# Expert rows turned by VectorE in 32x32 squares, gate and up products on column quarters, and a slot map made by products

## The reference, cut to what matters

```
M, D = 2080, 1024          # tokens, features;  w_gate, w_up: 1024x512;  w_down: 512x1024
gate = g_w * softmax(top_v);  expert = grp * 8 + top_i        # two experts for each token
# rows grouped by expert, each group padded to whole blocks
hdn = silu(xb @ w_gate[e]) * (xb @ w_up[e])                   # for each block xb of rows
yr  = hdn @ w_down[e]
out[token] += gate * yr[row of that token]
```

## Time and profile before

| | us |
|---|---|
| median of 3 runs | 3718.13 |
| lowest and highest | 3712.8, 3718.2 |
| profiled execution, its own time | 3718.09 |
| its span | 3716.3 |
| PE busy in the span | 2902.1 |
| DVE busy | 1572.8 |
| ACT busy | 1129.7 |
| POOL busy | 731.6 |

### The profile page before, as it was taken

The page is one execution under the profiler, slowest core; times in us unless marked ns, Lnnn a source line. Parts: engine busy times, 40 slices in busy tenths (PEclk is TensorE's granted clock), DMA queues, the critical chain, the costliest instruction groups (busy, mean ns, idle before and its releaser), DMA issues. The chain is left out here.

```text
span 3716.3 us, 44002 instructions
## 1 busy us (share of the span) xinstructions
PE 2902.1 (78%) x14656; PEld 1423.4 (38%) x14657; DVE 1572.8 (42%) x3624; ACT 1129.7 (30%) x2012; POOL 731.6 (20%) x858
## 2 busy tenths in 40 slices
PE   7999988925864657777774669992899999999940
PEld 3545353513432234555553434551333333333310
DVE  1145677886751578887643323332000000000025
ACT  1132452643431469865551211110111111111111
POOL 1404130301203323223314200003100000000024
PEclk9999999966777868889997779995999999999975
DMA  5011010002223101100006443321787668777747
GB/s 188 31 39 59 19 36 32 33 17 70 79 57 98 54 27 36 33 21 18 12 10 221 175 147 108 113 83 19 253 281 270 231 218 282 263 273 252 243 153 261
DMA packets 235196, 447.52 MB, mean 120 GB/s; under 512 B 49516, under 2 KB 86622, under 8 KB 235054
## 3 DMA queue, kind: packets, MB, share of 16 engines
q1 hardware_dynamic: 194158, 334.49, 26.4%
q0 software_dynamic: 27616, 89.49, 7.2%
q10 hardware_dynamic: 13280, 21.77, 1.8%
HBM read 359.98 MB, written 85.69 MB: 120 GB/s over the span
## 5 line engine op out<-in xcount | busy, mean ns | idle before, releaser
L773 PE MATMUL pj_cm<-pj_xT,pj_w 128*64 128x512 f32 (+1 forms) x1216 | 395.6, 600 | 5.8 <-ACT pj_xst L670 3.2
L2818 PE MATMUL ex_pgu<-ex_wgu,ex_xT 128*64 128x512 f32 x1344 | 297.7, 595 | 0.0
L2818 PE MATMUL ex_pgu<-pre_down_wgu,ex_xT 128*64 128x512 f32 x1312 | 293.2, 600 | 0.7 <-ACT ex_xT L2738 0.7
L2783 DVE TENSOR_TENSOR ex_hid<-ex_sg,ex_pgu 128x256 f32<-128x256 f32 x83 | 35.0, 421 | 596.6 <-ACT ex_sg L2742 596.6
L773 PEld LDWEIGHTS pj_cm<-pj_xT,pj_w 128*64 128x64 f32 (+1 forms) x1216 | 153.4, 163 | 240.4 <-issue 230.3
L2002 PE MATMUL ap_SB<-keep_kT,ap_qs 64*128 64x512 f32 (+3 forms) x640 | 169.2, 621 | 93.6 <-DVE ap_m L1934 74.7
L2013 PE MATMUL ap_TB<-keep_const,ap_L 128*128 128x128 f32 x1088 | 177.1, 306 | 69.2 <-ACT ap_PT L1795 48.5
L1783 ACT ACTIVATE ap_L<-ap_L,ap_nm 128x128 f32<-128x128 f32 (+15 forms) x128 | 153.2, 1197 | 174.1 <-DVE ap_nm L1939 170.4
L696 ACT ACTIVATE pj_U<-pj_sc,pj_cand 128x512 bf16<-128x512 f32 (+4 forms) x155 | 183.3, 1184 | 66.5 <-DVEq L517 66.4
L496 DVE TENSOR_SCALAR_CACHE_REDUCE pj_U<-pj_sc,pj_cand 128x384 bf16<-128x384 f32 (+9 forms) x182 | 194.7, 1103 | 14.2 <-issue 0.5
L2013 PEld LDWEIGHTS ap_TB<-keep_const,ap_L 128*128 128x128 f32 x1088 | 130.3, 153 | 149.5 <-ACT ap_L L1783 59.3
(11 more groups left out here) (521 smaller groups left out, 4790.9 us busy)
## 6 DMA issues: line engine op xcount, KB each, us to landing
pre_down_wgu<-in_w_gate SPq DMA_DIRECT2D x16, 2048.0 KB
pre_down_wgu<-in_w_up SPq DMA_DIRECT2D x16, 2048.0 KB
pre_down_wd<-in_w_down SPq DMA_DIRECT2D x16, 2048.0 KB, 8.9
ex_wgu<-in_w_gate SPq DMA_DIRECT2D x16, 2048.0 KB
ex_wgu<-in_w_up SPq DMA_DIRECT2D x16, 2048.0 KB
ex_wd<-in_w_down SPq DMA_DIRECT2D x16, 2048.0 KB
yslot<-ex_y ACTq DMA_DIRECT2D x166, 128.0 KB, 6.0
pj_x<-in_x_prompt SPq DMA_DIRECT2D x16, 512.0 KB, 5.1
```

Of the source, the lines that this page charges most:

```text
L773: mm = pe.matmul(cm[u % 2][cols * n:cols * n + cols, 0:width_], w[:, k, c0:c0 + cols], xT[:, k, 0:width_], start=(k == 0), stop=(k == KD - 1))
L2783: v.tensor_tensor(hid[:], sg[:], pgu[:, DE // 2:DE], ALU.mult).then_inc(sm["hid_ok"], 1)
L2818: mm = pe.matmul(pgu[BR * t:BR * t + BR, :], xT[:, k % 4, k // 4, :], wgu[par][:, k, :, 256 * t:256 * t + 256], start=(k == 0), stop=(k == ...
```

## The change

- **Layout of the normed rows.** `xn` is written by four `scalar_tensor_tensor` of 256 elements instead of one of 1024, with its features in another order, so that a quarter of a stored row holds the 32-wide pieces which one group of 32 partitions needs. `wr` is loaded by 16 transfers in the matching order instead of two. `w_down` is loaded by four transfers, one for each chunk, with its rows in another order.
- **Slot map.** The 34 scatters, the table `slot_tok` and its loads go. VectorE makes, for each of 34 columns of slots, a one-hot of the row in its block and a one-hot of the block, the latter times the token number. PE multiplies and sums them in 34 products, and VectorE makes the row numbers (eight small operations) from the result. Two small constant rows are loaded by SP.
- **Blocks.** POOL gathers 128 quarter rows of 1 KB twice for a block. VectorE turns them in 32x32 squares by one `transpose`, and the gated products by another, both from SBUF to SBUF. PE's transposes and ACT's two copies go. `gate_up` works on 32 rows at a time (`hh`), for each chunk four products of 32 stationary columns by 256 moving ones, one on each quarter of the array's columns; silu and the multiply work on these halves too. `down` keeps its eight products.

```
 def load_down(sp, io, buf, e, sem):
-    sp.dma_start(buf[:], io["w_down"][0, e].rearrange("(k p) f -> p k f", p=P)).then_inc(sem, 16)
+    rows = io["w_down"][0, e].rearrange("(q k j) f -> k q j f", q=4, j=32)
+    for k in range(DE // P):
+        sp.dma_start(buf[:, k, :], rows[k]).then_inc(sem, 16)
 (mix_out, SP)
-            sp.dma_start(wr[:, :, 0:NGRP], io["w_router_group"][0].rearrange("(k p) n -> p k n", p=P)).then_inc(sm["w_in"], 16)
-            sp.dma_start(wr[:, :, 8:LG], io["w_router_expert"][0].rearrange("(k p) n -> p k n", p=P)).then_inc(sm["w_in"], 16)
+            for c0, c1, name in ((0, NGRP, "w_router_group"), (8, LG, "w_router_expert")):
+                by_part = io[name][0].rearrange("(m c q j) n -> q m c j n", m=2, c=4, q=4)
+                for k in range(KD):
+                    sp.dma_start(wr[:, k, c0:c1], by_part[k // 2, k % 2]).then_inc(sm["w_in"], 16)
 (mix_out, POOL)
-            for t in range(NT):
-                rows = P if t < TILES else DEC
-                for k in range(2):
-                    pool.indirect_dma_start(io["slot_tok"], bass.IndirectOffsetOnAxis(ap=keep["slot"][0:rows, 2 * t + k:2 * t + k + 1], axis=0),
-                                            toki[0:rows, t:t + 1], None).then_inc(sm["scat"], 16)
-            pool.wait_ge(sm["scat"], 16 * 2 * NT)
 (mix_out, VectorE: one tile's xn, and the map)
-                    v.scalar_tensor_tensor(xn[r, par, :], xr[r, par, :], rstd[r, :], n2w[r, :], ALU.mult, ALU.mult).then_inc(sm["xn_ok"], 1)
+                    for q in range(4):
+                        part = lambda a_: a_.rearrange("p (k q j) -> p k q j", q=4, j=32)[:, :, q, :]
+                        ins = v.scalar_tensor_tensor(xn[r, par, 256 * q:256 * q + 256].rearrange("p (k j) -> p k j", j=32), part(xr[r, par, :]),
+                                                     rstd[r, :], part(n2w[r, :]), ALU.mult, ALU.mult)
+                    ins.then_inc(sm["xn_ok"], 1)
...
+            for c in range(2):
+                sl = slice(q * c, q * c + q)
+                v.tensor_tensor(onerow[:, sl, :], bc(rowio[:].unsqueeze(1), [P, q, BR]), bc(lowf[:, sl].unsqueeze(2), [P, q, BR]), ALU.is_equal)
+                for i in range(q * c, q * c + q):
+                    r = slice(0, rows_of(i // 2))
+                    v.tensor_scalar(oneblk[r, i, :], blkio[r, :], blkf[r, i:i + 1], keep["tok"][r, i // 2:i // 2 + 1], ALU.is_equal, ALU.mult).then_inc(sm["oh_ok"], 1)
+            v.wait_ge(sm["map_ok"], 1)
+            for q in range(4):
+                for hh in range(2):
+                    v.tensor_scalar(keep["rows"][32 * q:32 * q + 32, hh, 0:MAXBLK], pl[32 * hh:32 * hh + 32, 0:MAXBLK], 4.0, float(q), ALU.mult, ALU.add)
 (mix_out, PE)
+            for i in range(2 * NT):
+                r = slice(0, rows_of(i // 2))
+                pe.wait_ge(sm["oh_ok"], i + 1)
+                mm = pe.matmul(pl[0:BR, 0:MAXBLK], onerow[r, i, :], oneblk[r, i, :], start=(i == 0), stop=(i == 2 * NT - 1))
 (experts, POOL)
-                pool.indirect_dma_start(xg[:], None, halves, bass.IndirectOffsetOnAxis(ap=cur[:], axis=0)).then_inc(sm["xg_in"], 16)
+                for hh in range(2):
+                    pool.indirect_dma_start(xg[:, hh, :], None, quarters, bass.IndirectOffsetOnAxis(ap=cur[:, hh:hh + 1], axis=0)).then_inc(sm["xg_in"], 16)
 (experts, VectorE; a block is hidden(b), rows_done(b - 1), drain, turn_hidden(b))
+            def turn_rows(b):
+                v.wait_ge(sm["xg_in"], 32 * b + 32)
+                v.transpose(xT[:].rearrange("p k h t -> p h k t"), xg[:].rearrange("p h (k t) -> p h k t", t=32)).then_inc(sm["xt_ok"], 1)
             def hidden(b):
+                v.drain()
+                for hh in range(2):
+                    v.wait_ge(sm["sg_ok"], 2 * b + hh + 1)
+                    ins = v.tensor_tensor(hid[:, hh, :], sg[:, hh, :], pgu[hh][:, P:2 * P], ALU.mult)
+                ins.then_inc(sm["hid_ok"], 1)
+                turn_rows(b + 1)
+            def turn_hidden(b):
+                v.transpose(hT[:].rearrange("p k h t -> p h k t"), hid[:].rearrange("p h (k t) -> p h k t", t=32)).then_inc(sm["h_ok"], 1)
 (experts, PE; a block is gate_up(b), down(b - 1))
-                for k in range(KD):
-                    for t in range(2):
-                        mm = pe.matmul(pgu[BR * t:BR * t + BR, :], xT[:, k % 4, k // 4, :],
-                                       wgu[par][:, k, :, 256 * t:256 * t + 256], start=(k == 0), stop=(k == KD - 1))
+                for hh in range(2):
+                    for k in range(KD):
+                        for q in range(4):
+                            mm = pe.matmul(pgu[hh][32 * q:32 * q + 32, 0:2 * P], xT[:, k, hh, :],
+                                           wgu[par][:, k, :, P * q:P * q + P], start=(k == 0), stop=(k == KD - 1))
+                    mm.then_inc(sm["gu_ok"], 1)
```

More of the change, by code:

```diff
@@ L43 @@
 MAXBLK = 98
+SHIFT = BR.bit_length() - 1
 GROUP = 4
@@ L146 @@
 PICK, PK = picks()
+KEYROW = np.arange(MAXBLK, dtype=np.float32)[None, :].copy()
 SHIFTS = np.arange(BITS - 1, -1, -1)
@@ L2665, in experts @@
         wd = [keep["ew_d"], a.sb("wd", [P, DE // P, D])]
[L2666 to L2673 removed]
+        rows = keep["rows"]
+        cur = a.sb("cur", [P, 2], I32)
+        xg = a.sb("xg", [P, 2, D // 4])
+        xT = a.sb("xT", [P, KD, 2, 32])
+        sg = a.sb("sg", [P, 2, P])
+        hid = a.sb("hid", [P, 2, P])
+        hT = a.sb("hT", [P, DE // P, 2, 32])
         y = a.sb("y", [P, D // 2])
         zero = a.sb("zero", [BR, D])
[L2676 to L2677 removed]
+        pgu, py = [a.ps(f"pgu{n}") for n in range(2)], a.ps("py")
+        names = ("xg_in", "xt_ok", "gu_ok", "sg_ok", "hid_ok", "h_ok", "y_ok", "y_cp", "y_st", "zero_ok", "tail_st", "go")
         sm = {n: a.sem(n) for n in names}
@@ L2680, in experts @@
         block = a.block()
-        halves = io["xn2"].rearrange("r (h c) -> (r h) c", h=2)
+        quarters = io["xn2"].rearrange("r (q c) -> (r q) c", q=4)
         def over_blocks(eng, first, rest):
@@ L2699, in _ @@
         def _(sp):
-            for half in range(2):
-                sp.dma_start(slots[BR * half:BR * half + BR, :], io["slot_tok"].rearrange("(b p) o -> p (b o)", p=BR),
-                             allow_slow_non_contiguous=True).then_inc(sm["slot_in"], 16)
             for e in range(1, NEXP):
@@ L2793, in first @@
                     rows_done(b - 1)
+                v.drain()
+                turn_hidden(b)
             def rest(b, par):
@@ L2797, in rest @@
                 rows_done(b - 1)
+                v.drain()
+                turn_hidden(b)
+            turn_rows(0)
             over_blocks(v, first, rest)
@@ L2837, in down @@
                             mm.then_inc(sm["y_ok"], 1)
-            turn_rows(0)
             def first(b, par, j, begins):
@@ L2843, in first @@
                 gate_up(b, par)
-                turn_rows(b + 1)
                 if not begins:
                     down(b - 1, 1 - par)
-                turn_hidden(b)
-                pe.wait_ge(d_in[par], 16 * j + 16)
+                pe.wait_ge(d_in[par], 64 * j + 64)
                 pe.sem_inc(sm["go"], 1)
@@ L3014, in trunk_step @@
         with Alloc(nc, "pre") as b:
+            keep["rows"] = b.sb("rows", [P, 2, MAXBLK + 1], I32)
             keep["wo"], keep["wo_in"] = b.sb("wo", [P, KD, D]), b.sem("wo_in")
```

96 lines of the change are left out of this document (35 added, 61 removed).

## The result

The changed kernel takes 3997.1 us (median of 4 runs, 3985.5 to 4004.9) beside 3718.2 us of the kernel before on the same chip (3712.8 to 3724.2): a ratio of 1.075, 95% interval 1.072 to 1.078. The profiled execution has a span of 3996.9 us, 280.6 more than before. The forecast was 3800 us with a range of 3590 to 3890. It said slower, and so it came out, but the time lies 107 us above the range.

What follows compares the result with a forecast made beforehand. PE bounded the experts' stage before; after the change, four DMA engines carrying the down weights would set its pace, making block savings worthless. With earlier stage savings included, 3718 + 83 gave 3800 us, range 3590 to 3890.

Steps and rivals of the forecast that it cites:

- the four engines' rate: Experts' down weights: four engines at 25.5 GB/s each need 30.8 us an expert, stage +83 us; at 22.3 GB/s, +234.
- SP's later loads of tiles 2 and on: Mixing stage: these loads queue behind expert 0's weights but have some 18 us to spare, so no cost was counted.
- Router issues: Ahead of PE's first mixing work: sixteen router-weight transfers instead of two cost +6 us, bounds 2 and 15.
- Map 18 us: Last slot to experts' stage: one-hots and products replace scatters, 18 us (15 to 25) instead of 47.8, so -29.8.
- First product 11.5 us after the start: Head of the experts' stage: 11.5 us to the first product instead of 20.5, without table and PE's turn; -9 us.
- Block 10.59 us: PE's work per block in the experts' stage: 10.59 us, a saving of 0.97 each, -79.5 over 82 blocks.
- VectorE's turn 0.7: Each block's transposes on VectorE: 0.7 us taken, up to 2.8 possible; no cost while PE sets the pace.
- The gather costs nothing: Each block's two gather issues take 2.3 us and land after 3.5, hidden within more than 10 us.
- The time per product: Gate and up products: some 62 ns each would make 7.9 us and lose the gain; judged contradicted by a 27 ns row.
- Spread over 16 engines: Rival for the down weights: all sixteen engines carry them, PE sets the pace, -111 us, 3607 us; chance 0.22.
- It decides from eight engines on: Down weights: already with eight engines the queue needs 20.6 us and 3.5 an expert, below PE's 27.5.
- Share near 0.55: Sign in the experts' stage windows: DMA share near 0.55 with hardly a pause, four engines always busy.

Runs made afterwards that it cites:

- down_by_quadrant: Changed kernel with the down weights cut into one transfer per quarter of the partitions, outermost count 32 instead of four; 3636.8 us, ratio 0.975 to the kernel before.
- before_four_engines: Kernel before, given only the change's four down-weight transfers with outermost count four; 4011.6 us, ratio 1.076.
- down_twice: Changed kernel with gate and up loads left out from expert 2 on and the down weights loaded a second time instead; 4138.7 us, ratio 1.113.
- late_key_wait: Changed kernel with VectorE's wait for the two small constant rows moved from the mixing stage's head to the first compare; 3977.5 us, ratio 1.067.
- spread_best: Changed kernel with down weights by partition quarters, constant rows loaded before expert 0's weights, and their wait and PE's router-weight wait moved later; 3611.5 us, ratio 0.968.
- eight_wide: Changed kernel with down weights in four transfers over all 128 partitions, outermost count eight; 3690.5 us, ratio 0.989 to the kernel before.
- eight_engines: Changed kernel with down weights in sixteen transfers of eight partitions each, outermost count eight; 3886.6 us, ratio 1.045 to the kernel before.
- gate_up_by_act: Changed kernel with gate and up weights of experts 1 to 31 issued on ACT's queue instead of SP's; 4054.9 us, ratio 1.089.

## Why the prediction was wrong, step by step

*Right:* the sign, and where it turns. The down weights' transfers run on four engines (a share of 0.26), these are hardly ever without work (16 of 1220 us below a share of 0.20), and they set the pace (down_by_quadrant, before_four_engines). The rule of the Trainium skill that the prediction named (DMA: Bandwidth & Descriptors, section Why a DMA increments its semaphore by 16 and not by 1) names the number of engines by the slowest count, and these traces agree: a slowest count of four gave a share of 0.26, one of eight 0.53.

*The step that failed: the four engines' rate.* "At 25.5 GB/s that is 30.8 us", with 1.35 a block, gave 33.5 to 34.9 us an expert. Measured are 40.1, in place of 34.3 on average (30.8 + 2.6 x 1.35), and 31 x 5.8 = 180 of the 197 us by which the forecast missed. The bytes and the number of engines were right and the rate was mis-sized. 25.5 GB/s lies between the rates of two short stretches, 16 us and 1 us long, in which weights streamed on all engines. The four reach it only when gate and up are not loaded (25.5 in down_twice); beside them it is 21.7. A nearer number stood in the kernel before's table of queues, as a mean over the stage. With 22.15 an expert takes 39.6 us, so the stage 31 x 5.3 = 164 us more, and the forecast would have been 3965; with the 20 us of the next point, 3985. The prediction did give 22.3 GB/s its price, +234, but took the upper value. That 22.15 comes so near is in part luck: the same reckoning in the changed kernel gives 19.2 GB/s (193.41 MB at 51.7% of 1220 us), and 24.9 in down_twice.

*A wait that the sum has not.* "SP's later loads of tiles 2 and on queue behind expert 0's weights, and have a tile's time, some 18 us, to spare" looked at the loads and not at what waits for them. The diff makes VectorE wait at the stage's head for two loads that stand behind 6.29 MB: +20.3 us, of which late_key_wait gives back 20.5.

*The small terms.* Router issues +6: +5.5. Map 18 us: 15.0. First product 11.5 us after the start: 10.0. Block 10.59 us: 10.63, of it gate and up 7.05 (3837.32 - 3830.27) for 7.00. But the 79.5 us that the blocks were to save came to 65 with the deal mended (spread_best); where the others went wasn't traced. VectorE's turn 0.7: 0.71 for 512 columns and 0.45 for 256. The gather costs nothing. The time per product that the prediction weighed, by the Trainium skill (TensorE: Matmul & The Clock Gate, section Wait — 56ns, not 53.3ns?) some 62 ns, would have made gate and up 7.9 us; 128 records in 7.11 us are 56 ns each.

*The rivals.* "Spread over 16 engines", 3607 us, is near what the change is worth with the deal mended: 3637 us, and 3611 with the two waits at the mixing stage's head mended too. In the latter the terms are -32.8, -10.5 and -65 for the forecast's -29.8, -9 and -79.5, so misses of both signs went into the agreement. "It decides from eight engines on" was too light: eight cost 1.4% more than sixteen (55 us of waits for down weights). A likely reason, worked out and not tested, is that an expert of two blocks then has 21.3 us of PE's work for some 27 of transfers (0.524 MB / 22.15 + 3.2).

*The signs.* Share near 0.55: 0.62. PE's waits 100 to 200 us: 306. Issues 33 to 35 us apart: 40.1. First product near 2580: 2601.9, for the 7.5 us of the stages before and the 20.3 of the wait. Gate and up groups 6.8 us: 7.1. The clock is below 1.00 in places: 0.88 over the stage, 0.50 in the 4 us behind the wait that ends at 3234.04.

*Open.* Why the four fall to some 19.7 GB/s beside the others, why the gate and up packets are the ones that get longer, and why all engines then show as busy at 245 GB/s (a 2 KB packet takes 142 ns in that window). Why half of the down weights on four engines and half by quarters costs as much as three quarters on four: shown is only that transfers by quarters are slow themselves, not why.

## What to carry to other kernels

A cut of a transfer that changes neither its bytes nor its packets can still change how many engines carry it: look at the outermost count on both sides, and read the DMA share and the GB/s of a window together. For the pace of a queue that is never empty don't take the rate of the best stretch alone: the mean of a busy engine over the whole stage, MB divided by share, was the nearer one here, and the two together are bounds and not a constant. And for each wait that a change adds, ask what is issued ahead of the load that ends it.

## What the runs showed of the hardware

- The outermost count set the number of engines: four gave 98 GB/s at a share of 0.26 (changed kernel), eight 198 at 0.53 (eight_wide).
- The partitions of a transfer went with the rate of one engine: 24.8 GB/s to 128 partitions (eight_wide), 11.6 to eight (eight_engines). A 4 KB packet took 282 ns in transfers to 32 partitions (spread_best), for 190 in transfers to 128 (kernel before).
- An issue behind transfers that are still under way can hold its engine: 15 to 21 us for the four transfers of the down weights, where an issue with nothing before it took 0.4 to 0.6 us. On ACT's queue the up weights were issued in 0.59 us and the stores behind them in 17.5 (gate_up_by_act).
- Four engines carried 25.5 GB/s each when gate and up were not loaded (down_twice), and 21.7 when they were (changed kernel).
